# A routing stage rewritten between the mixer and the experts: norm by token columns, token table before gate table, last scalings on one engine

## The reference, cut to what matters

```
x = x + hybrid_mixer(rmsnorm(x, g_mix), ...)            # ends in merged @ w_out
xt = rmsnorm(x, g_ffn)
g_logits = xt @ w_rg + b_rg ; e_logits = xt @ w_re + b_re
# group = argmax(g_logits), 2 best experts of the group's 8,
# gate  = softmax(group) * p_k / (p_1 + p_2)
# each token's row goes to its 2 experts of 32, in blocks of 128 rows
yb = silu(xb @ w_gate[e]) * (xb @ w_up[e]) @ w_down[e]
x = x + sum over the token's 2 rows of gate * yb
x = rmsnorm(x, g_final)
... second block, two layers ...
return rmsnorm_2(x, final_g)
```

## Time and profile before

| | |
|---|---|
| median of 3 runs | 3407.12 us (3405.99 to 3411.69) |
| the profiled execution | 3409.59 us, its span 3407.7 us |
| busy share | TensorE 98%, its weight load 81%, VectorE 63%, ScalarE 47%, GpSimd 6% |
| granted TensorE clock, mean | 0.991 |
| DMA | 492.94 MB, mean 145 GB/s |

### The profile page before, as it was taken

The page is one execution under the profiler, slowest core; times in us unless marked ns, Lnnn a source line. Parts: engine busy times, 40 slices in busy tenths (PEclk is TensorE's granted clock), DMA queues, the critical chain, the costliest instruction groups (busy, mean ns, idle before and its releaser), DMA issues. The chain is left out here.

```text
span 3407.7 us, 55618 instructions
## 1 busy us (share of the span) xinstructions
PE 3335.2 (98%) x23758; PEld 2765.4 (81%) x23758; DVE 2140.3 (63%) x2641; ACT 1585.9 (47%) x1844; POOL 200.0 (6%) x191
## 2 busy tenths in 40 slices
PE   8999999999999998999999999999999999999998
PEld 6987676878888887888888888888778888788886
DVE  6665553469888987665657663554576668753544
ACT  5432111248778884343356543434443355643432
POOL 0000000001101112000011000000000010000000
PEclk9999999999999999999999999999999999999999
DMA  5211541369999996122111111344122111111433
GB/s 221 83 54 55 172 163 67 138 242 404 414 414 416 413 415 256 57 75 87 39 64 57 39 63 50 133 151 142 57 86 70 45 45 57 38 63 50 156 124 110
DMA packets 97244, 492.94 MB, mean 145 GB/s; under 512 B 10920, under 2 KB 11432, under 8 KB 59104
## 3 DMA queue, kind: packets, MB, share of 16 engines
q1 hardware_dynamic: 77216, 417.31, 32.0%
q0 software_dynamic: 14160, 51.55, 4.3%
q10 hardware_dynamic: 5616, 20.45, 1.5%
HBM read 431.43 MB, written 57.84 MB: 144 GB/s over the span
## 5 line engine op out<-in xcount | busy, mean ns | idle before, releaser
L136 PE MATMUL ps<-HH,WS 128*128 128x512 f32 (+1 forms) x2592 | 1035.3, 399 | 9.2 <-DVE WS L1572 7.1
L138 PE MATMUL ps<-HH,WS 128*128 128x512 f32 (+1 forms) x2592 | 1014.2, 391 | 0.0
L137 PE MATMUL ps<-HL,WS 128*128 128x512 f32 (+1 forms) x1952 | 763.8, 391 | 0.0
L136 PEld LDWEIGHTS ps<-HH,WS 128*128 128x128 f32 (+1 forms) x2592 | 487.7, 188 | 118.1 <-DVE WS L1572 11.9
L138 PEld LDWEIGHTS ps<-HH,WS 128*128 128x128 f32 (+1 forms) x2592 | 487.2, 188 | 106.0
L1637 ACT ACTIVATE WA<-ps 128x512 f32<-128x512 f32 x240 | 142.7, 595 | 840.8 <-PE ps L138 817.4
L137 PEld LDWEIGHTS ps<-HL,WS 128*128 128x128 f32 (+1 forms) x1952 | 368.1, 189 | 74.5 <-issue 1.2
L136 PE MATMUL ps<-WAR 128*128 128x512 f32 x768 | 306.9, 400 | 0.9 <-DVE WAR L1366 0.9
L138 PE MATMUL ps<-WAR 128*128 128x512 f32 x768 | 301.2, 392 | 0.0
L1572 DVE TENSOR_TENSOR WS<-RAW,WS 128x1024 fp32r<-128x1024 f32 (+1 forms) x153 | 201.7, 1318 | 122.7 <-ACT WS L1567 122.7
L136 PE MATMUL ps<-WS,HH 128*128 128x256 f32 x896 | 259.6, 290 | 14.3 <-DVE WAR L2561 12.5
(11 more groups left out here) (409 smaller groups left out, 5218.8 us busy)
## 6 DMA issues: line engine op xcount, KB each, us to landing
WR<-in_weu SPq DMA_DIRECT2D x36, 1024.0 KB, 9.1
WR<-in_wed SPq DMA_DIRECT2D x36, 1024.0 KB, 8.9
WR<-in_weg SPq DMA_DIRECT2D x35, 1024.0 KB, 10.4
RAW<-in_wo SPq DMA_DIRECT2D x32, 1024.0 KB, 4.9
WA<-in_wada SPq DMA_DIRECT2D x48, 512.0 KB, 4.5
H<-in_weg SPq DMA_DIRECT2D x23, 1024.0 KB, 10.4
H<-in_weu SPq DMA_DIRECT2D x23, 1024.0 KB, 8.9
H<-in_wed SPq DMA_DIRECT2D x22, 1024.0 KB, 10.1
```

The costliest lines, as they stand in the source:

```text
L136: t.matmul(o, l[0], r[0], start=st, stop=False)
L137: t.matmul(o, l[0], r[1], start=False, stop=False)
L138: return t.matmul(o, l[1], r[0], start=False, stop=sp)
```

## The change

It has seven edits.

1. The norm of half 1 is made as token columns. VectorE adds the last square too (`vector_square_added(v, "ffn", 7, 1)`), TensorE makes four one-column sums (`tensor_columns`), ScalarE makes the root on 128x4 (`scalar_columns_root`) straight into `rcol`. The two 512-column sums, the root on 128x512, the four turns of line 864 and the copy of line 858 go, for half 1.
2. The rank matmuls run in the rounded format: `OH` and a copy of the strict triangle are written as fp32r, and `ones_rounded` is used.
3. The table is made in two parts of 48 columns, in two banks. `hot` and the token part of `places` come first, `tab_ix` follows; then the gates (`pg` to `gates`), the gate part of `places`, and a second matmul `gated`. `away` is made after `hot`.
4. The bounds move from routing into the projection (half 0, m = 0, 3, 6) and share one exp and ln.
5. The splits of expert 0 move. Piece 0 on VectorE goes ahead of the last `x_mix`; piece 1 on ScalarE goes behind the root, on VectorE behind the block table; pieces 2 and 3 on VectorE go behind the split of the gathered rows.
6. The matmuls nobody reads: 4, 3, 6 become 2, 2, 4.
7. The last scalings are all on VectorE; ScalarE's two, GpSimd's two and their semaphores go, and the stores go in order.

```diff
-            brief("scale", 1, end=("row_scale", 1))
+            brief("scale", 1, end=("columns_ln",))
...
-            brief("table", end=("tab_gate",))
+            brief("table", end=("route", "tok"))
+            brief("gated", end=("tab_gate",))
...
+        def tensor_columns(t):
+            sq = square_of("ffn", 7, 1)
+            free(t, banks, "scale", 1)
+            t.wait_ge(*at("sq_added", "ffn", 7, 1))
+            for c in range(4):
+                o = t.matmul(ps("scale", 1)[:, c:c + 1], sq[:, c * 128:(c + 1) * 128], ones[:, 0:1], start=True, stop=True)
+            o.then_inc(*up("scale_mm", 1))
+        def scalar_columns_root(a):
+            rcol = views()["rcol"][:, 4:8]
+            table_for(a, ACT.Ln)
+            a.wait_ge(*at("row_scale", 0))
+            a.wait_ge(*at("scale_mm", 1))
+            a.activation(rcol, ps("scale", 1)[:, 0:4], ACT.Ln, scale=1.0 / 1024, bias=eps).then_inc(*up("columns_ln"))
+            a.wait_ge(*at("columns_ln"))
+            a.activation(rcol, rcol, ACT.Exp, scale=-0.5).then_inc(*up("columns_root"))
...
         def moe_tensor(t):
             tensor_scores(t, 6)
-            tensor_square_sums(t, "ffn", 1)
-            tensor_row(t, 0)
             tensor_scores(t, 7)
-            tensor_row(t, 1)
-            tensor_row_scale(t, 1)
-            for c in (2, 3, 4):
+            tensor_columns(t)
+            for c in range(5):
                 tensor_row(t, c)
-            tensor_warm(t, 0, 4)
+            tensor_warm(t, 0, 2)
...
-            t.matmul(b[:, 0:288], strict, OH, start=True, stop=False)
+            t.matmul(b[:, 0:288], before, OH, start=True, stop=False)
...
-            tensor_warm(t, 1, 3)
+            tensor_warm(t, 1, 2)
+            for part, nm in enumerate(("table", "gated")):
+                free(t, banks, nm)
+                for k in range(2):
+                    t.wait_ge(*at(("hot", "hot_gate")[part], k))
+                    for c in range(8):
+                        at_ = c * 96 + part * 48
+                        o = t.matmul(ps(nm)[:, 0:48], c8(tl("hot", k))[:, c, :], tl("places", k)[:, at_:at_ + 48],
+                                     start=(k, c) == (0, 0), stop=(k, c) == (1, 7))
+                o.then_inc(*up(("tab_mm", "tab_gate_mm")[part]))
-            tensor_warm(t, 2, 6)
+            tensor_warm(t, 2, 4)
...
             scalar_expert_split(a, 0, 0)
+            square(7, 1)
+            scalar_columns_root(a)
             scalar_expert_split(a, 0, 1)
-            square(7, 1)
-            scalar_root(a, "ffn", 1)
...
                 for k in range(8):
-                    if not (i and k in ON_GPSIMD):
-                        vector_normed(v, X, "fin", k, i, p2(0, "fin", k))
+                    vector_normed(v, X, "fin", k, i, p2(0, "fin", k))
```

More of the change, by code:

```diff
@@ L327, in token_half, with plan_squares @@
             return slice(i * 512, (i + 1) * 512)
-        def plan_squares(tag, i, held=False):
+        def plan_squares(tag, i, columns=False):
             for j in range(4):
                 wa.take("sq", tag, i, j)
-            banks.take("rms", tag, i)
-            if not held:
+            if not columns:
+                banks.take("rms", tag, i)
                 banks.give(("rms", tag, i), ("rms_ln", tag, i))
@@ L338, in plan_squares @@
                 else:
-                    wa.give(("sq", tag, i, j), ("sq_summed", tag, 7, i))
+                    wa.give(("sq", tag, i, j), ("scale_mm", 1) if columns else ("sq_summed", tag, 7, i))
         def square_of(tag, k, i):
@@ L513, in moe_plan @@
             wa.give(("r", "ffn"), ("hT_turn", 7, 1))
-            wa.give(("EH",), ("hot", 1))
+            wa.give(("EH",), ("hot_gate", 1))
             for k in range(2):
-                wa.give(("hot", k), ("tab_mm", k))
-                wa.give(("places", k), ("tab_mm", k))
+                wa.give(("hot", k), ("tab_gate_mm",))
+                wa.give(("places", k), ("tab_gate_mm",))
             loose_pieces()
@@ L1042, in moe_tensor @@
                 tensor_row(t, c)
-            tensor_warm(t, 1, 3)
-            free(t, banks, "table")
-            for k in range(2):
-                t.wait_ge(*at("hot", k))
-                for c in range(8):
-                    o = t.matmul(ps("table")[:, 0:96], c8(tl("hot", k))[:, c, :], tl("places", k)[:, c * 96:(c + 1) * 96],
-                                 start=(k, c) == (0, 0), stop=(k, c) == (1, 7))
-                o.then_inc(*up("tab_mm", k))
-            tensor_warm(t, 2, 6)
+            tensor_warm(t, 1, 2)
[9 more added lines that the diff above has]
+            tensor_warm(t, 2, 4)
             def start(j):
@@ L1350, in moe_vector @@
                 *up("route", "tok"))
-            v.tensor_scalar(V["tab"][:, 48:96], ps("table")[:, 48:96], 1.0, None, ALU.mult).then_inc(*up("tab_gate"))
+            v.wait_ge(*at("route_exp", "ge"))
+            v.tensor_reduce(V["pg"], V["ge"], AX, ALU.add).then_inc(*up("route", "pg"))
+            v.wait_ge(*at("route", "pg"))
+            v.reciprocal(V["pg"], V["pg"]).then_inc(*up("route", "pgr"))
+            v.wait_ge(*at("route_exp", "ex"))
+            v.tensor_scalar(den, ex, 1.0, None, ALU.add).then_inc(*up("route", "den"))
+            v.wait_ge(*at("route", "den"))
+            v.reciprocal(den, den).then_inc(*up("route", "denr"))
+            v.wait_ge(*at("route", "denr"))
+            v.tensor_tensor(GT[:, 0, :], V["pg"], den, ALU.mult).then_inc(*up("route", "gt0"))
+            v.wait_ge(*at("route", "gt0"))
+            v.tensor_tensor(GT[:, 1, :], GT[:, 0, :], ex, ALU.mult).then_inc(*up("gates"))
+            v.wait_ge(*at("gates"))
+            for k in range(2):
+                places = tl("places", k)[:, 0:768].rearrange("p (c n) -> p c n", n=96)
+                jj = EH[:, k * 384:(k + 1) * 384].rearrange("p (c n) -> p c n", n=48)
+                v.tensor_tensor(places[:, :, 48:96], jj, GT[:, k, :].unsqueeze(2).broadcast_to([128, 8, 48]), ALU.mult).then_inc(
+                    *up("hot_gate", k))
+            vector_gains(v)
             v.tensor_scalar(V["NBK"], pend[:, 31:32], 32.0, None, ALU.add).then_inc(*up("n_blocks"))
@@ L3387, in mixer_plan @@
                     banks.take("logit")
-                    plan_squares("ffn", 1, held=True)
+                    plan_squares("ffn", 1, columns=True)
                 for m in range(8):
@@ L3471, in mixer_scalar @@
                         scalar_root(a, "ffn", 0)
+                    if i == 0 and m == 3:
+                        bounds_scalar(a)
                     if m:
@@ L3501, in mixer_vector @@
                         vector_square_added(v, "ffn", m - 1, i)
+                    if i and m == 7:
+                        vector_expert_split(v, 0, 0)
                     xs = X[:, m, token_half(i)]
@@ L3510, in mixer_vector @@
                         vector_router(v)
+                    if i == 0 and m == 0:
+                        bounds_vector(v, 0)
+                    if i == 0 and m == 6:
+                        bounds_vector(v, 1)
                     if i and m == 5:
@@ L4449, in result_sync @@
             else:
-                for k in (0, 1, 4, 2, 3, 5, 6, 7) if i else range(8):
-                    s.wait_ge(*(at("normed_gpsimd", k) if i and k in ON_GPSIMD else at("normed", "fin", k, i)))
+                for k in range(8):
+                    s.wait_ge(*at("normed", "fin", k, i))
                     s.dma_start(out[k * 128:(k + 1) * 128, token_half(i)], X[:, k, token_half(i)]).then_inc(*up("stored", k, i, by=16))
```

100 lines of the change are left out of this document (35 added, 65 removed).

## The result

The change makes the kernel slower. It took 3413.39 us in the median of 20 runs (3406.11 to 3418.21), the kernel before 3407.32 us in the median of 20 beside it (3401.88 to 3414.01): a ratio of 1.0017, 95% interval 1.0011 to 1.0023, some 6 us. The forecast was 3403.8 us with a range of 3399.5 to 3409.5. The profiled execution took 3413.41 us, its span 3411.5 us; busy shares are those of before within a point, the mean granted clock is 0.987 (0.991).

A forecast was written before the change was run, and what follows sets the result against it. TensorE, busy 98% of the span, was taken as the bound, with the stage's stores as the gather's last wait; stage -2.5 and end -0.8 gave -3.3 us, from the median 3407.1 to 3403.8 us, range 3399.5 to 3409.5.

The forecast's parts named there:

- Norm by columns, ranks: Early routing: logits scaled at 709.3 instead of 712.40 us, ranks at VectorE at 718.3 instead of 722.2.
- Stores: Ahead of the first `hot`: stores of chunks 2 and 3 land at 731 us, 3.5 us later than before.
- The table: Routing: first `hot` to end of token table 5.7 us instead of 6.8; token part read at 736.8, 0.6 later.
- The clock rival: Routing tables: TensorE's 4.6 us idle halves the table matmuls' speed, 1.9 to 3.4 us later, about 3406.4; chance 0.35.
- the late-store rival: Ahead of `hot`: stores of chunks 2 and 3 land near 737, 3410 us, or 3412 with cold clock; chance 0.12.
- The clock at the experts: First expert matmuls: TensorE busy up to the turn keeps the clock at 2.4 GHz, giving 3.0 us back.
- Sum of the stage: Routing to experts: start 0.5 us later, 3.0 us back from the clock, together -2.5 us.
- The splits: Expert 0's pieces 2 and 3, split behind the gathered rows: ready before they are wanted, no cost.
- the bounds: Inside the projection: they ride in waits of VectorE and ScalarE where TensorE sets the pace, costing nothing.
- the end: Last scalings: eight on VectorE take 5.4 to 5.6 us where six took 6.17; -0.8 us taken.
- The range: Total time: 3399.5 to 3409.5 us, given as 8 in 10.

The follow-up runs named there:

- e3: The changed kernel with the four loads into `H` held until the stores of chunks 2 and 3 have landed; 3406.5 us, ratio 1.0000.
- e7: The changed kernel with 7 instead of 2 matmuls that nobody reads ahead of the first table matmul; 3409.3 us, ratio 1.0001.
- e4: The changed kernel with the gates made ahead of `hot` again and one table of 96 columns; 3407.3 us, ratio 1.0003.
- e14: The changed kernel, loads into `H` held until the first gathered rows landed, 1 instead of 4 idle matmuls behind the gates table; 3405.71 us, ratio 0.9988.
- e11: The kernel before, untouched, profiled once more; 3409.1 us, ratio 1.0002.
- e2: The changed kernel with ScalarE's split of expert piece 1 back ahead of the last square; 3408.1 us, ratio 1.0002.
- e10: e8 with 11 instead of 4 matmuls that nobody reads ahead of the turn of the gathered rows; 3401.83 us, ratio 0.9980.
- e9: e8 with the loads into `H` held until the first gathered rows landed and 6 instead of 4 idle matmuls; 3399.59 us, ratio 0.9970.
- e6: The kernel before with the four loads into `H` held until the last pair of stores has landed; 3409.3 us, ratio 1.0006.
- e8: The changed kernel with the edits of e2 and e4 and the held loads of e6 together; 3406.4 us, ratio 0.9995.
- e12: The kernel before with all last scalings on VectorE and the loads into `H` held until the first gathered rows landed; 3404.07 us, ratio 0.9989.
- e5: The changed kernel, untouched, run once more; 3411.9 us, ratio 1.0013.
- e1: The kernel before with only the last scalings all moved to VectorE; 3405.28 us, ratio 0.9994.

## Why the prediction was wrong

*Norm by columns, ranks.* Right. Logits 4.1 behind `x_mix` (forecast 4.2), ranks 13.1 (forecast 13.2), eight rank matmuls in 0.97 us where sixteen took 2.38.

*Stores.* Right: first copy 5.7 behind `x_mix` (forecast 6.1), `hot` behind a wait for the store at 731.39 (forecast 731, though with `x_mix` 2.15 sooner); ScalarE held by chunk 1 until 723.61 (723). SyncE's load behind the last stores was issued at 738.58 (stores at 737). e3 shows the cause by removing it.

*The table: this step failed.* The prediction says "the matmuls are as many: 5.7", and for the gates "the second table matmul (2 x 1.9)", both from 2.02 us of the earlier trace rows. They are as many for each pass, but at half the clock a half takes 3.5 us. From the first `hot` to the first expert matmul the forecast had 17.0 us; it took 25.2. By piece: `hot` to token part read 8.9 (5.8), from there to the end of the gates table 9.1 (5.6), idle matmuls 5.0 (3.6), turn to expert 2.4 (2.0). The clock rival had the place and the mechanism, but its price of 1.9 to 3.4 us covers one table at half speed. Both were: TensorE was busy 6.96 of 8.40 us around the first table and stayed at 0.50 through the second. e7 shows the price for the first table (2.8 to 3.4 us in A), e4 that of the second pass and of the gates behind `hot` (4.6 to 5.2 in B). What lets the clock fall is not settled: in e3 and e14 it fell within the first table with no wait ahead. The measured 3413.4 us lie in the range of the late-store rival (3408 to 3415), but not by its mechanism, as the stores landed when the forecast had them.

The Trainium skill (TensorE: Matmul & The Clock Gate, What's actually happening) says that the throttled state is the default and activity releases it. The fall agrees: after 4.22 us without work the clock was 0.50. The page's sentence gives no time for the release; here TensorE had been busy with the tables for 14 us, between two waits, before the clock rose at 752.3, within the idle matmuls.

*The clock at the experts.* Right in kind: no wait for the gather, 1.00 at the first expert matmul. From there to the fold it took 566.5 us instead of 570.5 (569.8 in e11), 3.3 to 4.0 back where 3.0 were forecast.

*Sum of the stage:* 49.4 - 42.5 - 4.0 = +2.9 us where the forecast had -2.5.

*The splits, the bounds, the end.* The splits cost nothing, as forecast. The bounds: the last `x_mix` comes at 703.7 to 707.2 us in all profiles, in the mean at 704.7 in the five with the old order and at 705.9 in the eleven with the new. A short stretch of low clock near 660 us, with 1.7 us lost in it, is in nine of the eleven traces and in two of the five. That is too few to say whether the edits in the projection bring it on; the forecast had nothing for it. The end was undersized: 2.1 us, not 0.8. The eight scalings are as sized (5.39 us); the sum took what they save (0.8) for the whole, but the span ends with the stores, not with the scalings. SyncE issues the first store 0.8 us behind the first scaling instead of 1.9, the 1.1 that the prediction names and leaves out of its sum, and from there to the end it is 7.2 us instead of 8.2 (the eight issues take 4.97 instead of 5.43). The order of the stores and GpSimd's part were not tried apart.

*The range.* By the prediction's own chances 3399.5 to 3409.5 holds 0.875, not 8 in 10; the measured time is above it either way.

*What stays open.* The parts give +2.9 - 2.1 = +0.8 us between the two profiles, and the profiles differ by 3.8: 2.15 were lost ahead of `x_mix`, where the change's trace has two more short stretches of low clock than that of before, and 0.8 between the fold and the first of the last scalings, in code that the change leaves alone. The medians differ by 6.1. Up to 2 us of that may be what e11 shows: its stage is 2.2 us shorter than in the profile that the forecast was made from, and if most executions are like it, the forecast was made against a slow stage. The last 2 to 3 us were not found; e2, with the same stage, had 3408.13 on its chip. Single profiles of the same kernel lie up to 8.5 us from the median of its runs (e10: 3410.30 against 3401.83; e9: 3406.87 against 3399.59), so sums from one profile each are not sharper than that.

## What to carry to other kernels

When a chain is shortened, ask first which transfer its last wait is for, and whether the shortening itself starts other transfers sooner: here four loads that could wait another 24 us took the DMA engines from the stores, and when they were moved only a little (e6, e8), from the gather. One changed line that let them wait gave 4 to 7 us in B to either order (e3, e12). A step that is split into two passes on an engine pays its price twice, here at half the clock each time; price matmuls that stand behind a wait at both levels.

## What the runs showed of the hardware that was not expected

- The table matmuls at the 2.4 GHz level take 3.67 us for 32 (e7), at 1.2 GHz 7.04; in e3 and e14 they began without a wait ahead and the group still took 4.35 and 4.10. The gates table, behind a wait of 2.1 us, took 7.03 to 7.04 us in every profile that had one (the change, e2, e3, e5, e7, e14).
- A short wait does not decide by itself whether the clock falls: behind 1.75 us ahead of the table in e8 it stayed at 1.00, behind 1.74 in e9 and e10 it fell within the table, with the same instructions up to there. Each is one execution.
- A gather's instruction on GpSimd took 1.04 us when it began ahead of VectorE's split of 128x2048 (e11) and 2.97 when it began inside one; in e1, e4, e6, e7 and e12 one that ran beside such a split took 2.75 to 2.84. The Trainium skill (SBUF — State Buffer, Who interferes with whom) reports a probe in which `tensor_tensor` did not stall a DMA, and has a VectorE instruction with two inputs in SBUF contend with a GpSimd instruction that reads SBUF; these rows show the issue of a gather three times as long beside one, but not by which port.
- The loads into `H` could be issued at 33.3 us behind `x_mix` (e9) instead of 9.0 (before), and no expert waited for them.
